# Hybrid decoder layer: the last state update left out, the square root's table called behind the last silu

## The reference

```python
def step(state, inp):
    q_c, k_c, u_c, w_c, g_c, qk_c = inp
    v_new = u_c - w_c @ state
    o = (q_c * jnp.exp(g_c)[..., None]) @ state + qk_c @ v_new
    g_last = g_c[..., -1]
    k_dec = k_c * jnp.exp(g_last[..., None] - g_c)[..., None]
    state = state * jnp.exp(g_last)[..., None, None] + jnp.einsum('bhcd,bhce->bhde', k_dec, v_new)
    return state, o

_, o = lax.scan(step, state0, xs)
...
o = rmsnorm(o, out_norm) * jax.nn.silu(z.reshape(bsz, s_len, GDN_HEADS, GDN_DV).astype(jnp.float32))
...
o_nsa = nsa_group(...)
return jnp.concatenate([o_gdn, o_nsa], axis=-1) @ w_out
```

## Time and profile before

| | us |
|---|---|
| median of 3 runs | 1116.54 |
| lowest, highest | 1116.14, 1116.83 |
| the profiled execution, device time | 1116.19 |
| its span in the profile | 1114.4 |
| busy: PE | 1082.6 |
| busy: PE weight load | 938.2 |
| busy: DVE | 778.0 |
| busy: ACT | 446.5 |
| busy: POOL | 443.5 |

### The profile page before, as it was taken

The page is one execution under the profiler, slowest core; times in us unless marked ns, Lnnn a source line. Parts: engine busy times, 40 slices in busy tenths (PEclk is TensorE's granted clock), DMA queues, the critical chain, the costliest instruction groups (busy, mean ns, idle before and its releaser), DMA issues.

```text
span 1114.4 us, 20141 instructions
## 1 busy us (share of the span) xinstructions
PE 1082.6 (97%) x8484; PEld 938.2 (84%) x8484; DVE 778.0 (70%) x941; ACT 446.5 (40%) x639; POOL 443.5 (40%) x281
## 2 busy tenths in 40 slices
PE   6899999999999999999999999999999999999996
PEld 5799899988998888887787667888898899989986
DVE  5998379946987566653566487566997389837964
ACT  6534244423435334311214566343453145413432
POOL 0663169505833000312300389433480279306912
PEclk9999999999999999999999899999999999999999
DMA  6244233333232222113103001123133323422222
GB/s 228 77 124 151 76 94 99 116 108 103 89 112 95 87 103 76 40 58 134 39 28 86 4 1 39 36 79 103 59 104 115 111 77 114 135 92 80 101 85 76
DMA packets 34590, 98.45 MB, mean 88 GB/s; under 512 B 3664, under 2 KB 10320, under 8 KB 32848
## 3 DMA queue, kind: packets, MB, share of 16 engines
q1 hardware_dynamic: 34224, 97.26, 26.7%
q10 hardware_dynamic: 288, 0.08, 0.0%
HBM read 95.24 MB, written 2.10 MB: 87 GB/s over the span
## 4 chain that ended last, share of the span: by engine, by line
PE 87%; DVE 8%; ACT 3%; issue 2%; DMA 0%; POOL 0%; DVEq 0%; ACTq 0%
PE bank L592 25%; PE bank L594 24%; PE bank L593 24%; PE bank L2131 3%; PE bank L1917 1%; PE bank L1884 1%; PE bank L1905 1%; DVE hb_lo L716 1%; DVE w_lo L1020 1%; PE bank L2183 1%; DVE cv L1611 1%; DVE w_lo L1097 1%; PE bank L2180 1%; PE bank L1716 1%; PE bank L1520 1%
## 5 line engine op out<-in xcount | busy, mean ns | idle before, releaser
L592 PE MATMUL bank<-hb_hi,w_hi 128*128 128x256 f32 x1064 | 295.5, 278 | 6.9 <-DVE w_lo L1097 3.6
L594 PE MATMUL bank<-hb_hi,w_lo 128*128 128x256 f32 x1064 | 294.7, 277 | 0.0
L593 PE MATMUL bank<-hb_lo,w_hi 128*128 128x256 f32 x1064 | 294.7, 277 | 0.0
L592 PEld LDWEIGHTS bank<-hb_hi,w_hi 128*128 128x128 f32 x1064 | 200.5, 188 | 8.7 <-DVE w_lo L1097 4.5
L593 PEld LDWEIGHTS bank<-hb_lo,w_hi 128*128 128x128 f32 x1064 | 200.5, 188 | 0.3
L594 PEld LDWEIGHTS bank<-hb_hi,w_lo 128*128 128x128 f32 x1064 | 200.6, 189 | 0.0
L592 PE MATMUL bank<-act_hi,w_hi 128*128 128x512 f32 (+1 forms) x460 | 180.4, 392 | 10.0 <-DVE w_lo L1033 9.8
L593 PE MATMUL bank<-act_lo,w_hi 128*128 128x512 f32 (+1 forms) x460 | 179.8, 391 | 0.0
L594 PE MATMUL bank<-act_hi,w_lo 128*128 128x512 f32 (+1 forms) x460 | 179.6, 391 | 0.0
L1014 ACT ACTIVATE w_hi<-raw 128x1536 fp32r<-128x1536 f32 (+1 forms) x67 | 108.7, 1622 | 161.1 <-PE bank L594 161.1
L1020 DVE TENSOR_TENSOR w_lo<-raw,w_hi 128x1536 fp32r<-128x1536 f32 (+1 forms) x67 | 159.2, 2376 | 15.8 <-ACT w_hi L1014 15.3
(11 more groups left out here) (307 smaller groups left out, 1702.6 us busy)
## 6 DMA issues: line engine op xcount, KB each, us to landing
raw<-in_gate_up SPq DMA_DIRECT2D x43, 1024.0 KB, 5.4
raw<-in_w_in SPq DMA_DIRECT2D x13, 1024.0 KB, 4.9
raw<-in_down SPq DMA_DIRECT2D x8, 1024.0 KB, 5.1
raw<-in_down SPq DMA_DIRECT2D x16, 512.0 KB, 4.1
raw<-in_down SPq DMA_DIRECT2D x8, 768.0 KB, 4.3
raw<-in_w SPq DMA_DIRECT2D x8, 512.0 KB, 3.8
x<-in_x SPq DMA_DIRECT2D x4, 512.0 KB, 7.5
raw<-in_w_out SPq DMA_DIRECT2D x4, 512.0 KB, 4.6
```

Of the source, the lines that this page charges most:

```text
L592: pe.matmul(out_ap, wh, xh, start=first, stop=False)
L593: pe.matmul(out_ap, wh, xl, start=False, stop=False)
L594: return pe.matmul(out_ap, wl, xh, start=False, stop=last)
```

## The change

In the delta rule the job `s1` of the last tile is left out, with its three parts: POOL's decay, PE's product and DVE's addition. PE's wait in slot 1 counts one state less. On ACT, behind the last silu, a square root of one column is put, which nothing reads; the program puts the table load ahead of it.

```diff
-    back = [[(TT - 2, n) for n in r] for r in BACK] + [[(TT - 1, n) for n in r] for r in BACK]
+    last = BACK[:-1] + (["o"],)
+    back = [[(TT - 2, n) for n in r] for r in BACK] + [[(TT - 1, n) for n in r] for r in last]
     return out + back
...
             if kind == "z":
                 act.wait_ge(proj_evac, CONV_EVACS + n - 3)
                 act.activation(z[:, n - 10, :], z[:, n - 10, :], ACT.Silu).then_inc(z_silu, 1)
+                if n == HALVES_N - 1:
+                    act.activation(root_first, eps_col, ACT.Sqrt)
...
             if i == 1:
-                pe.wait_ge(state_ready, 2 * TT + 1)
+                pe.wait_ge(state_ready, 2 * TT)
                 pe.wait_ge(o_ready, TT)
...
             elif name in ("vn0", "vn1"):
                 c = int(name[2])
+                if (n, c) == (TT - 1, 1):
+                    return
                 pool.wait_ge(state_ready, 2 * n + c + 1)
```

## The result

| | us |
|---|---|
| before, median of 7 runs (lowest, highest) | 1116.24 (1111.92, 1117.00) |
| after, median of 7 runs (lowest, highest) | 1111.63 (1110.11, 1114.64) |
| ratio after / before | 0.9964 [0.9948, 0.9980] |
| the profiled execution of after (span) | 1114.64 (1112.8) |

The change gains more than the 1.1 us forecast. Over all 19 executions of after the median is 1113.6 and the mean 1112.8. Of before, 84 executions were timed beside the experiments; one at 1125.55 stands alone and is left out here. Over the other 83 the median is 1116.4 and the mean 1116.2 (with the seven of the table the mean is 1116.1).

A forecast was written before the change was run, and what follows sets the result against it. PE, busy 1082.6 of 1114.4 us, bounds the kernel, so only its stand at the recurrence's end counts. Two gains of 1.08 overlap to 1.1 off: 1115.1 from the profiled execution, 1115.4 from the median; range 1112.9 to 1117.0.

The forecast's parts named there:

- Path of the change: Last projection to first exponentials: update's 1.08 us and table load's 1.08 don't add, since ACT becomes late; gain 1.1.
- the chain: Waits from the last projection's end at 621.60 to the exponentials at 628.69, said to run in line through four engines.
- Rivals on that path: Moved load exposed on ACT, 0.2 us lost, 1116.7, chance 0.04; the two gains add, 2.2 off, 1114.3, chance 0.02.
- Idle: PE's wait for the first exponentials ahead of attention's third slot: moves about 1.1 us earlier, stays near 1.66 us long.
- the low stretch: Ten microseconds at 1.2 GHz in attention shortly behind PE's idle, priced at 4.4 us; the forecast kept it as it was.
- The step that failed: Argument against the clock rival: before's times lie within 0.7 us, so attention's low clock stretch is stable.
- gone: Rival case: attention's low clock stretch vanishes, another 4.4 us off, 1111.0; chance 0.07.
- The rival: PE's clock in attention: low stretch gone 0.07, shorter 0.12, longer by one or two thirds 0.07, as much again 0.03.
- The free-running clock gate: PE's clock window doesn't start with the kernel, so a 1.1 us shift would change nothing on average; sum does without it.

The follow-up runs named there:

- after_delay: The changed kernel with five matmuls of zeros ahead of the last third of the last projection; 1116.29 us (12 runs), ratio 0.9995 to before.
- before_delay: The kernel before with ten matmuls of zeros ahead of the last third of the last projection; 1115.75 us (12 runs), ratio 0.9994 to before.

## Why the prediction was right, and where it was wrong

- **Path of the change: right.** Squares start 625.70 - 622.89 = 2.81 us behind the projection's end on ACT (forecast 624.44 - 621.60 = 2.84), the root 627.20 - 622.89 = 4.31 (4.35), the exponentials 5.93 (6.0) and 628.82 - 624.27 = 4.55 behind the silu's end (4.6). The gain is 1.16; each part alone gives 1.09; they don't add, because the load sits on ACT, which waits for the projection through z. One slip of reading: the chain runs through three engines, PE, DVE and ACT, and not four.
- **Rivals on that path: fallen.** The load wasn't exposed. It took 1.28 and the next ACTIVATE began 1.30 behind its start (624.29 to 625.59). The Trainium skill, page "ScalarE: Activation LUTs", section "What ACT_TABLE_LOAD costs", adds a drain of some 1380 ns; this trace has no room for it here either.
- **Idle: right in size** (1.60), **and taken for harmless.** I worked out that PE's idle stays as long and concluded that what follows it stays as well. With an idle as long, the share of executions with the low stretch went from most (about 1 by the index, 0.86 by the count) to about 0.4.
- **The step that failed** is "the times of before lie within 0.7 us (1116.14 to 1116.83), which speaks for a stable stretch", with 0.07 for its going. By it the sum put the clock's part at nothing and came to 1115.4, where 1111.63 was measured first and 1113.6 over all executions. The runs showed about 2 us of gain from the clock beside the 1.16 of the path. Three executions can't show that a state which comes in most executions comes in all; 83 of before reach from 1111.9 to 1120.0. And I treated "gone" as one case for the kernel, all or nothing. It is a matter of each execution, so the median can lie anywhere between the two. The rival was named and priced, 4.4 us, and measured 4.0; its chance was wrong.
- **The free-running clock gate.** The Trainium skill, page "TensorE: Matmul & The Clock Gate", "Part 1: The HAM clock gate", says that the gate's window runs free and doesn't start with the kernel. The traces agree: the clock's moments lie elsewhere against the program in each execution (first rise at 12.71 to 15.99). What I drew from it, that a shift changes nothing on average, isn't borne out as it stands: L of `after_delay` and after differ by 7.1. The dense matmuls that make the shift may do it. Or the moments are spread unevenly against the idle by the time the program comes there, since each low stretch ahead of it holds the program up. No run here settles which. A low stretch ahead of attention begins at 458.6 to 465.0 in twelve of the 14 traces, and that is no fixed time either: all 14 have an idle of 2.64 to 2.71 us on PE there, and in the twelve the clock falls from 0.6 us ahead of the idle's end to 0.7 behind it.
- **Open as well:** whether `before_delay`'s lower L is the place alone, since ten zero matmuls also lengthen the dense stretch ahead; and whether the other low stretches, with L of 14.7 left, can be had off. The profiles without the one in attention have two to five of them, one of them always in the last 9 us of the kernel.

## What to carry over

Near a place where PE has an idle of a microsecond or two among small matmuls, read the granted clock behind it, and ask how often it falls, not whether: take the clock of many executions, not the trace of one. If a low stretch follows, the first edit to try is to shorten or fill that idle. Here five matmuls of zeros gave 3.8 us with no shorter path, and the table load moved alone, which gives 1.09 us of path and cuts the idle by 1.1, gave 5.9. And an edit that must be compared may not move tensors: give it memory that is already there.

## What the runs showed of the hardware

- An idle of 1.6 us on PE, with small matmuls around it, is followed by ten microseconds at 1.2 GHz in some executions and not in others (five of seven traces); at 0.4 to 0.6 us no kernel's mean shows it (L 14.5 to 14.8), at 2.5 us all of it (L 26.8).
- The moments at which the clock changes keep their distances within an execution (before and `after_delay`: 0.90, 0.89, 0.89 and 0.90 apart at 13, 392, 460 and 631 us), and lie elsewhere against the program in each.
- Time at the low clock costs less than half of it: over all executions, each against its kernel's mean, 0.33 us of time per microsecond of L, and 4.0 / 10.2 = 0.39 in attention, where POOL is busy 9.16 of 10 us at the full clock.
- The place of the tensors alone, moved by one unused tensor of ten fp32 columns, changes the mean record of the 256-column matmuls from 278 to 284 ns and that of the costliest group of 512-column ones from 399 to 393 (the 393 and 388 above are mixed with another shape), in all 6.5 us.
